# The first half of the first weights is issued by ScalarE, SyncE's first transfers are those of x, and two small row loads move down SyncE's queue

## What is computed

```
hp = rmsnorm(xp, norm_mix[i])          # i = 0
hs = rmsnorm(xs, norm_mix[i])
bg, cg, xv = jnp.split(h @ w_in, 3, axis=-1)      # w_in: 1024 x 3072
conv, new_hist = causal_dwconv(cg * xv, hist, conv_w)
mixer = (bg * conv) @ w_out
...
convffn: (silu(causal_dwconv(h @ w_gate, hist, conv_w) + conv_b) * (h @ w_up)) @ w_down
```

## Time and profile before

| | |
|---|---|
| time, median of 3 runs | 1195.93 us (1195.52 to 1196.65) |
| the profiled execution's own time | 1196.42 us |
| its span in the profile | 1194.9 us |
| PE busy | 1187.7 us, 99% of the span |
| DVE, ACT busy | 775.0 us, 546.6 us |
| granted TensorE clock | 1.00 of full speed (2.4 GHz) in all 40 slices |

### The profile page before, as it was taken

How to read it: one execution, slowest core, us unless ns; L and a number is a source line. 1 busy time by engine, 2 the same in 40 slices (tenths; PEclk the granted TensorE clock), 3 DMA queues, 4 the chain that set the end, 5 groups by cost and what they waited for, 6 DMA issues and landing times.

```text
span 1194.9 us, 26317 instructions
## 1 busy us (share of the span) xinstructions
PE 1187.7 (99%) x10352; PEld 1138.7 (95%) x10352; DVE 775.0 (65%) x1424; ACT 546.6 (46%) x956; POOL 21.1 (2%) x50
## 2 busy tenths in 40 slices
PE   8999999999999999999999999999999999999998
PEld 8999999999999999999999999988999999999998
DVE  6766677767777644445676776868887776774333
ACT  6333345444544432225466565556654454442221
POOL 0000000000000000000000000000000000000000
PEclk9999999999999999999999999999999999999999
DMA  8355535655444545455467766669544455446542
GB/s 222 107 181 153 176 110 166 177 169 176 151 150 137 171 153 161 143 171 172 150 210 202 212 179 191 194 161 240 148 148 153 137 172 154 150 146 183 132 115 44
DMA packets 285909, 193.19 MB, mean 162 GB/s; under 512 B 40433, under 2 KB 282153, under 8 KB 284678
## 3 DMA queue, kind: packets, MB, share of 16 engines
q1 hardware_dynamic: 282636, 137.04, 41.9%
q0 software_dynamic: 1792, 54.43, 12.8%
q10 hardware_dynamic: 1402, 0.61, 0.2%
HBM read 184.52 MB, written 64.16 MB: 208 GB/s over the span
## 4 chain that ended last, share of the span: by engine, by line
PE 94%; DVE 3%; ACT 1%; issue 1%; DMA 1%; SPq 0%; DVEq 0%
PE acc L2012 22%; PE acc L1994 16%; PE acc L2016 12%; PE acc L2014 11%; PE acc L2013 11%; PE acc L2015 11%; PE acc L2050 3%; PE N L1981 1%; PE M L2050 1%; PE N L2305 1%; PE M L1981 1%; PE acc L2285 1%; PE M L2254 1%; DVE wl L1294 1%; DVE u L1791 1%
## 5 line engine op out<-in xcount | busy, mean ns | idle before, releaser
L886 ACT ACTIVATE wh<-wraw 128x1024 fp32r<-128x1024 f32 (+1 forms) x211 | 217.9, 1033 | 275.3 <-PE acc L2016 176.4
L1294 DVE TENSOR_TENSOR wl<-wraw,wh 128x1024 fp32r<-128x1024 f32 (+1 forms) x211 | 252.9, 1198 | 130.4 <-ACT wh L886 102.8
L2012 PE MATMUL acc<-h_both,wh 128*128 128x512 f32 x832 | 315.6, 379 | 0.0
L2016 PE MATMUL acc<-h_both,wl 128*128 128x264 f32 x832 | 231.3, 278 | 0.0
L2014 PE MATMUL acc<-h_both,wh 128*128 128x264 f32 x832 | 229.6, 276 | 0.0
L2013 PE MATMUL acc<-h_both,wh 128*128 128x264 f32 x832 | 229.6, 276 | 0.0
L2015 PE MATMUL acc<-h_both,wl 128*128 128x256 f32 x832 | 226.8, 273 | 0.0
L2014 PEld LDWEIGHTS acc<-h_both,wh 128*128 128x128 f32 x832 | 157.2, 189 | 22.4
L1994 PE MATMUL acc<-h_both,wh 128*128 128x256 f32 (+2 forms) x1152 | 178.1, 277 | 0.2
L2012 PEld LDWEIGHTS acc<-h_both,wh 128*128 128x128 f32 x832 | 159.7, 192 | 0.1
L2013 PEld LDWEIGHTS acc<-h_both,wh 128*128 128x128 f32 x832 | 157.2, 189 | 0.0
(11 more groups left out here) (288 smaller groups left out, 1726.2 us busy)
## 6 DMA issues: line engine op xcount, KB each, us to landing
out_dram<-in_cache_kv_d_dram POOLq DMA_DIRECT2D x24, 1364.0 KB, 6.3
wraw<-in_ffn_w_gate_dram SPq DMA_DIRECT2D x44, 512.0 KB, 3.9
wraw<-in_ffn_w_up_dram SPq DMA_DIRECT2D x44, 512.0 KB, 3.9
wraw<-in_attn_w_qkv_dram SPq DMA_DIRECT2D x36, 512.0 KB, 4.1
out_dram<-in_cache_kv_d_dram POOLq DMA_DIRECT2D x8, 2044.0 KB, 8.2
wraw<-in_ffn_w_down_dram SPq DMA_DIRECT2D x32, 448.0 KB, 3.9
wraw<-in_sc_w_in_dram SPq DMA_DIRECT2D x23, 512.0 KB, 3.9
wraw<-in_ffn_w_down_dram SPq DMA_DIRECT2D x16, 512.0 KB, 4.2
```

Of the source, the lines that this page charges most:

```text
L886: nc.scalar.activation(wh[c % 2][:, 0:k], wraw[:, c % 4, 0:k], ACT.Copy).then_inc(hi_done, 1)
L1294: V.tensor_tensor(wl[c % 2][:, 0:k], wraw[:, c % 4, 0:k], wh[c % 2][:, 0:k].bitcast(F32), ALU.subtract).then_inc(split_done, 1)
L2012: T.matmul(wide, h[:, k, :], wide_pairs(both[:, :, k0 + k]), start=start, stop=False)
L2016: ins = T.matmul(rest, l[:, k, :], paired(high, 1, CUT), start=False, stop=stop)
```

## The change

ACT's third issue becomes w0, and its two row loads go to SP, behind the first three weight chunks. SP no longer issues w0. On ACT, the scaled high half of tile 0 now comes before the high half of w0.

```
-            sp.dma_start(wraw[:, 0, 0:DK // 2], w[:, 0:DK // 2, 0:P]).then_inc(half_loaded, 16)
             sp.dma_start(xin[:, :, P:2 * P], x_tok[:, :, P:2 * P]).then_inc(x_in[1], 16)
             sp.dma_start(wraw[:, 0, DK // 2:DK], w[:, DK // 2:DK, 0:P]).then_inc(chunk_loaded[0], 16)
...
             for c in range(1, 4):
                 load_in(0, c)
+            sp.dma_start(rows[0:2 * DK, 0, :], norm_ffn.rearrange("l (k p) -> (l k) p", p=P)) \
+                .then_inc(gain_rows_in, 16)
+            sp.dma_start(rows[2 * DK:5 * DK, 0, :], sc_conv_w.rearrange("l j (k p) -> (l j k) p", p=P)) \
+                .then_inc(gain_rows_in, 16)
...
             act.dma_start(mix_rows, norm_mix.rearrange("l (k p) -> (l k) p", p=P)).then_inc(mix_rows_in, 16)
-            act.dma_start(rows[0:2 * DK, 0, :], norm_ffn.rearrange("l (k p) -> (l k) p", p=P)) \
-                .then_inc(gain_rows_in, 16)
-            act.dma_start(rows[2 * DK:5 * DK, 0, :], sc_conv_w.rearrange("l j (k p) -> (l j k) p", p=P)) \
-                .then_inc(gain_rows_in, 16)
+            act.dma_start(wraw[:, 0, 0:DK // 2], kmajor(sc_w_in[0])[:, 0:DK // 2, 0:P]).then_inc(half_loaded, 16)
...
+            act.wait_ge(params_ready, 1)
+            x_high(0)
             act.wait_ge(half_loaded, 16)
             nc.scalar.activation(wh[0][:, 0:DK // 2], wraw[:, 0, 0:DK // 2], ACT.Copy).then_inc(hi_first, 1)
-            act.wait_ge(params_ready, 1)
-            x_high(0)
             x_high(1)
```

## The result

The changed kernel takes 1199.02 us (median of 11 runs, 1196.54 to 1201.42) against 1195.83 us before (11 runs, 1195.22 to 1197.15): a ratio of 1.0025, 95% interval 1.0017 to 1.0032. It is slower by about 3 us, outside the range that was given, on a side that had been given a chance of 0.04. The profiled execution took 1198.96 us, its span is 1197.4 us, 2.5 us more than before.

The account below looks back on a forecast made before the run. The prediction took x2's landing and PE's 1185 us of work after it as the bound. Its terms, -0.07 + 0 + 0 + 0 us, gave 1196.35 for the profiled execution, written as 1195.8 for the median; range 1194.4 to 1197.1.

Parts of the forecast that it names:

- What bounds the kernel: Opening: x2's landing starts tile 2 on PE at 10.18 us, and that plus 1185 us of work sets the end.
- the earlier issue: x2 on SP's queue, issued 0.55 us earlier: gains only 0.07 us, at best 1.3 us, at worst 0.
- The terms for ScalarE's order and the two row loads: Cast of w0 behind tile 0's high half, and row loads moved to SP: each costs 0 us.
- the landing of w0: Opening, ACT's queue: w0, issued at 2.23 us, lands at 6.4, between bounds of 5.7 and 8.7.
- Rival B: Opening: w0 late, costing its landing minus 7.9, 0.8 us at 8.7; chance 0.09 under 2.4 us, 0.01 over.
- the 7.9: Latest landing of w0 in us that costs nothing: 3.0 us of ACT's operations must precede x_high(2) at 10.88.
- decides only from 10.3 on: Late w0 makes the kernel slower by over 2.4 us only if it lands at 10.3 us or later.
- Rival C: TensorE's clock falls to 1.2 GHz, each us of PE's work costing up to one more; chance 0.02.
- unless w0 is late: PE's pause is split, before 7.5 and before 10.1 us, neither part longer except with late w0.
- The other two routes to a loss, rows and order: Moved rows holding up PE at 28.75 or chunk 4 at 30.45, chance 0.01; ACT's new order, cost 0.

Follow-up runs that it names:

- e4: Changed kernel, but SyncE issues w0 second as before, leaving only the moved row loads and ScalarE's new order: 1195.84 us, ratio 0.9999.
- e7: Kernel before, all transfers as they were, but ScalarE's cast of w0 also waits for w1: 1199.31 us, ratio 1.0021.
- e9: The e7 kernel with 8 unused constant products on TensorE behind the transposes of tile 1: 1197.50 us, ratio 1.0011.
- e10: Kernel before with 5 constant products on TensorE just ahead of the transposes of tile 2: 1196.55 us, ratio 1.0004.
- e3: Kernel before with one edit, w0 issued third on ScalarE's queue, row loads and order of work unchanged: 1200.18 us, ratio 1.0036.
- e2: Changed kernel with 8 unused constant products on TensorE behind the transposes of tile 1: 1197.24 us, ratio 1.0009.
- e6: Changed kernel, but SyncE issues x2 and all behind it only when w0 has landed: 1198.12 us, ratio 1.0016.
- e5: Changed kernel with w0 first in ScalarE's queue, ahead of the sample and norm_mix rows: 1199.12 us, ratio 1.0022.
- e1: Changed kernel, but SyncE issues w0 itself, third, behind x0 and x1: 1195.85 us, ratio 0.9998.

## Why the prediction was wrong

**What bounds the kernel** was right for the profiled execution: x2 landed at 10.2 in both, and PE's work behind its start in the opening sets the end. That the two landings agree to 0.04 us is partly luck. x2 landed at 8.94, 9.02, 9.74, 10.14 and 10.14 in the five profiles in which SyncE issues w0 second and x2 behind w1 (the kernel before, e4, e7, e9, e10), and at 9.18, 9.41 and 10.18 in the three with w0 third on ScalarE's queue and x2 not held. No gain from the earlier issue shows, as the prediction had it, but PE doesn't always wait for x2: in e4 tile 2 started at 9.57, with x2 there since 9.02. The terms for ScalarE's order and the two row loads were right (1195.84 us with these alone).

**The step that failed is the landing of w0.** The prediction took 6.4 us, as if w0 were "served in turn with x1 and w1", and gave 8.7 as the upper bound, "it is the last of the four 256 KB transfers". It measured 9.3 in the changed kernel, 8.5 in e3 and 8.45 in e2. It was not served in turn: by 5.0 us it had moved some 24 of its 256 KB, and x1 and most of w1 went ahead of it. And the bound counted four transfers only. It left out that x2, issued 0.36 us after w0 on the other queue, moves beside what is left of w0; when w0 landed, 0.9 MB of x2 to x4 had already moved. One queue doesn't keep later transfers out either: 0.8 MB of x2 to x4 had moved when w1 landed at 8.66 in the kernel before. But w0 stood second there, and when it landed, at 5.0, none of them had moved. The share of 0.76 at 4 to 5 us, against 1.07 in the earlier trace rows, is no mark of the second queue: e7, with the old queues, shows 0.85 and 212 GB/s there.

**The price of lateness fits as far as it went.** Rival B said landing minus 7.9, so 0.6 us for a landing at 8.5 and 1.4 at 9.3; without the clock's part the loss is 1.3 us (1197.24 against 1195.92), and the one run of the changed kernel at full clock lost 0.7. The landings in those runs are not known, though, and the 7.9 comes from an execution in which x2 landed at 10.14; where x2 lands near 9, lateness costs from an earlier time on. And B stopped there, with "decides only from 10.3 on".

**The clock was priced alone, not as what follows from B.** Rival C had the right price, up to a us for each us of work: 3.4 us at half speed do 1.7 us of work, and cost 1.7. It had a chance of 0.02, since PE's pause would be no longer "unless w0 is late". That condition was then not carried on. w0 was late, PE's pause before its first product was 2.41 us in the profile, where the longest before had been 1.35, and 10 of 11 runs of the changed kernel had a clock under 1.000. It makes 1.8 us of the 3, shown twice with the constant products. The pause's length alone doesn't tell whether the clock falls: it fell at 1.57 us in e7, and not at 1.48 us in the profile of e6, where 3 of 10 runs had a clock under 1.000. The other two routes to a loss, rows and order, are excluded by experiment.

## What to carry to other kernels

On a second queue a transfer shares the DMA engines with everything that the first queue issues, behind it as well as ahead, so don't bound its landing by the bytes ahead of it; here second place in one queue gave 5.0 us, third on the other queue 8.45 to 9.3. A landing read from one profile is one draw: w1 and x2 moved by 1.2 to 1.5 us between executions with the same first issues. Before an opening is reordered, price a late operand together with what the longer pause does to TensorE's clock: the two came as one here, about 1.3 and 1.8 us. Where the weights must be late, constant products in the pause bought back the clock's part.

## What the hardware showed unexpectedly

A transfer of 256 KB took 3.8 us as the first on ScalarE's queue, 6.2 to 7.0 us as the third with x2 beside it, 5.1 us without x2. On SyncE's queue it took 3.5 us as the second and 5.0 as the third. The Trainium skill, page "DMA: Bandwidth & Descriptors", section "Issuing engines are not separate DMA queues", says that a second issuer saves only the issue time; the runs agree that it brings no bandwidth (from 2 to 8 us 265 GB/s in the changed kernel, 285 before), and add that it can cost the moved transfer 2.7 to 3.5 us of landing.

The moment at which TensorE first reached full speed varied between executions with the same first products, and was latest, about 13.4 us, in e5, where PE had first waited for `norm_mix`. In the profile with w0 second on SyncE (the rows and the order alone) the first transposes of x took this long, against 0.66 us in other profiles:

```profile
5.91 1.11 PE L1981 MATMUL M<-ident,big 128*128 128x128 f32 x4
```

That execution took 1195.84 us all the same, this kernel's median: tile 2 started at 9.57 in it and at 9.56 in e1, whose transposes were fast, and chunk 4's cast at 29.78, the earliest of all profiles. So slow products that early need not cost anything. The clock column shows 1.00 there, so in the first microseconds the durations tell more than that column.
